# Expert steps of a streaming encoder kernel: six equal matmul pieces per row block, turns on VectorE, two neighbouring down rows per partition

## What is computed

```python
def swiglu(h, wg, wu, wd):
    g = jnp.einsum('btd,df->btf', h, wg)
    u = jnp.einsum('btd,df->btf', h, wu)
    return jnp.einsum('btf,fd->btd', jax.nn.silu(g) * u, wd)

def moe(h, router, wg, wu, wd):
    logits = jnp.einsum('btd,de->bte', h, router).astype(jnp.float32)
    vals, idx = lax.top_k(logits, TOP_K)
    gates = jax.nn.softmax(vals, axis=-1)
    comb = jnp.sum(jax.nn.one_hot(idx, N_EXPERTS, dtype=jnp.float32) * gates[..., None], axis=-2)
    for e in range(N_EXPERTS):
        out = out + comb[..., e:e + 1].astype(h.dtype) * swiglu(h, wg[e], wu[e], wd[e])
```

## Time and profile before

| | us |
|---|---|
| median of 3 runs | 1261.35 (1259.78 to 1263.61) |
| the profiled execution's own time | 1260.88 |
| its span, first to last instruction | 1259.0 |
| PE busy | 1235.7 (98%) |
| DVE busy | 316.3 (25%) |
| ACT busy | 303.8 (24%) |
| 277 MB of expert weights begin to be used at | 517 |
| one step of the loop, from SP's issues | 91.5 |

### The profile page before, as it was taken

How to read it: one execution, slowest core, us unless ns; L and a number is a source line. 1 busy time by engine, 2 the same in 40 slices (tenths; PEclk the granted TensorE clock), 3 DMA queues, 4 the chain that set the end, 5 groups by cost and what they waited for, 6 DMA issues and landing times.

```text
span 1259.0 us, 30642 instructions
## 1 busy us (share of the span) xinstructions
PE 1235.7 (98%) x13657; PEld 909.0 (72%) x13657; DVE 316.3 (25%) x640; ACT 303.8 (24%) x594; POOL 79.0 (6%) x175
## 2 busy tenths in 40 slices
PE   8999999999999999999999999999999999999998
PEld 5476699999975656667677676676676676675775
DVE  1677544444326566200000000000000000000002
ACT  2566533333334654200100100100101101001001
POOL 4231000000001020000000000100100100000100
PEclk9999999999999999999999999999999999999999
DMA  8261385544050632999999999999999999999991
GB/s 293 50 164 34 101 267 168 167 151 165 20 197 1 128 102 88 390 394 408 398 382 404 398 379 394 394 382 393 390 381 395 386 388 396 386 387 389 384 365 52
DMA packets 124224, 349.70 MB, mean 278 GB/s; under 512 B 8400, under 2 KB 33840, under 8 KB 124096
## 3 DMA queue, kind: packets, MB, share of 16 engines
q1 hardware_dynamic: 118896, 335.55, 72.1%
q0 software_dynamic: 3648, 10.60, 3.0%
q10 hardware_dynamic: 1552, 1.56, 0.4%
HBM read 339.65 MB, written 8.04 MB: 276 GB/s over the span
## 4 chain that ended last, share of the span: by engine, by line
PE 92%; DVE 3%; DMA 2%; ACT 2%; issue 1%; SPq 0%; DVEq 0%; ACTq 0%
PE ps L2307 33%; PE ps L2312 22%; PE ps L2219 11%; PE ps L1963 8%; PE ps L2235 5%; DMA ring<-in_w_in 2%; PE ps L2332 1%; PE ps L2036 1%; PE ps L2044 1%; PE ps L2096 1%; PE ps L2111 1%; PE ps L2149 1%; PE ps L2159 1%; PE ps L1976 1%; PE ps L2060 1%
## 5 line engine op out<-in xcount | busy, mean ns | idle before, releaser
L2307 PE MATMUL ps<-ring,xg 128*32 128x512 f32 (+2 forms) x2688 | 279.1, 465 | 7.4 <-issue 7.4
L2312 PE MATMUL ps<-ring,xg 128*32 128x256 f32 (+1 forms) x1344 | 276.5, 365 | 0.0
L2307 PE MATMUL ps<-ring_more,xg 128*32 128x512 f32 (+2 forms) x1920 | 196.6, 454 | 0.0
L2312 PE MATMUL ps<-ring_more,xg 128*32 128x256 f32 (+1 forms) x960 | 193.6, 358 | 0.0
L2312 PEld LDWEIGHTS ps<-ring,xg 128*32 128x32 f32 x1344 | 147.5, 110 | 37.0 <-issue 0.2
L2307 PEld LDWEIGHTS ps<-ring,xg 128*32 128x32 f32 x2688 | 118.7, 110 | 48.3 <-issue 14.0
L1762 DVE TENSOR_TENSOR act_m<-sgm,ps 128x768 f32<-128x768 f32 x24 | 22.9, 954 | 473.6 <-PE ps L2312 473.6
L2312 PE MATMUL ps<-ring_more,am 128*32 128x256 f32 x636 | 140.1, 379 | 0.0
L2307 PE MATMUL ps<-ring_more,am 128*32 128x512 f32 (+1 forms) x1272 | 139.8, 486 | 0.0
L2312 PEld LDWEIGHTS ps<-ring_more,xg 128*32 128x32 f32 x960 | 103.6, 110 | 27.7
L1963 PE MATMUL ps<-ring,hT 128*128 128x512 f32 x256 | 115.3, 596 | 0.1
(11 more groups left out here) (360 smaller groups left out, 1570.1 us busy)
## 6 DMA issues: line engine op xcount, KB each, us to landing
ring<-in_moe_w_up SPq DMA_DIRECT2D x48, 1024.0 KB, 11.6
ring_more<-in_moe_w_down SPq DMA_DIRECT2D x48, 1024.0 KB, 8.7
ring<-in_moe_w_gate SPq DMA_DIRECT2D x32, 1024.0 KB, 8.2
ring_more<-in_moe_w_gate SPq DMA_DIRECT2D x32, 1024.0 KB, 9.4
ring<-in_moe_w_down SPq DMA_DIRECT2D x32, 1024.0 KB
ring_more<-in_moe_w_gate SPq DMA_DIRECT2D x32, 768.0 KB, 9.6
ring<-in_moe_w_up SPq DMA_DIRECT2D x32, 768.0 KB, 7.6
ring_more<-in_moe_w_up SPq DMA_DIRECT2D x16, 1024.0 KB, 8.0
```

The lines of the kernel that those rows point to most:

```text
L2307: ins = mm_(ps[GRAN * g:GRAN * g + GRAN, b + c0 // 512, 0:c1 - c0], x[:, GRAN * g:GRAN * g + GRAN], w[:, c0:c1], start=first, stop=last)
L2312: ins = mm_(ps[SLOTS:P, b + c0 // 512, at_:at_ + tail], x[:, GRAN * g:GRAN * g + GRAN], w[:, main:main + tail], start=(first and g == here ...
```

## The change

- **Pieces.** `granules` takes the place of `lanes` for gate, up and, in the loop, down. Each row block gets six matmuls of the same length (half the chunk's columns: 512, or 384 in chunk 2). Granules 0 and 1 have two quarters each, one for each half of the columns, all in one bank (`fixed`). Granule 2's two halves go to the next bank (`shared`), on quarters 0 and 1 for even row blocks and on 2 and 3 for odd ones, so that two partial sums stand in four quarters. Over two row blocks each tile streams 1536 columns, as before. The last step's down stays with `lanes`.
- **Partial sums.** ACT copies the upper half of granule 2's partial sum to SBUF (`gate_part`, `up_part`, `y_tail`), DVE adds the lower one (`gates`, `activations`, `output`), and silu and product run in two pieces.
- **Turns.** `turn_chunk` and `turn_rows` are gone from PE, and the copies behind them from ACT and DVE. DVE writes `am` and `xg` with 32x32 transposes, SBUF to SBUF: 12 a chunk (`turned`) and 12 for the tokens (`tokens`), of 32 partitions by 256 elements (192 in chunk 2).
- **Down rows.** Partition p now holds hidden rows p·nk to p·nk+nk-1 of a chunk (nk is 8, in chunk 2 it is 6), so the two row blocks of a unit are one run of 8 KB for each partition. The transposes read `act_m` with a step of nk to match.

```diff
+                def granules(b, x, w, half, n, n_last):
+                    def fixed():
+                        for s_ in range(4):
+                            g, h = s_ // 2, s_ % 2
+                            ins = mm_(ps[GRAN * s_:GRAN * s_ + GRAN, b, 0:half], x[:, GRAN * g:GRAN * g + GRAN], w[:, half * h:half * h + half],
+                                      start=(n == 0), stop=(n == n_last))
+                        return ins
+                    def shared():
+                        for h in range(2):
+                            r0 = GRAN * (2 * (n % 2) + h)
+                            ins = mm_(ps[r0:r0 + GRAN, b + 1, 0:half], x[:, GRAN * 2:SLOTS], w[:, half * h:half * h + half],
+                                      start=(n < 2), stop=(n >= n_last - 1))
+                        return ins
+                    if n % 2:
+                        shared()
+                        return fixed()
+                    fixed()
+                    return shared()
...
-                    k0 = CW // P * c + sum(KUNIT[c][0:h])
-                    src = a["moe_w_down"][0].rearrange("e (k p) n -> p (e k) n", p=P)[:, bass.ds(e * FT + k0, n), :]
+                    k0 = sum(KUNIT[c][0:h])
+                    chunk = a["moe_w_down"][0, bass.ds(e, 1), CW * c:CW * c + WIDTH[c], :]
+                    src = chunk.rearrange("o (p k) n -> p (o k) n", k=nk)[:, k0:k0 + n, :]
...
 # ACT
-                    A(sgm[:, 0:ACT_W[c]], wide(0)[:, 0:ACT_W[c]], ACT.Silu).then_inc(silu_done, 1)
+                    A(sgm[0:HALF, BANK:BANK + w], ps[HALF:P, 1, 0:w], ACT.Copy).then_inc(gate_part, 1)
+                    A(sgm[:, 0:w], ps[:, 0, 0:w], ACT.Silu)
+                    act.wait_ge(gate_sum, j * CHUNKS + (c + 1))
+                    A(sgm[0:HALF, BANK:BANK + w], sgm[0:HALF, BANK:BANK + w], ACT.Silu).then_inc(silu_done, 1)
...
 # DVE
+                    V.tensor_tensor(part, part, ps[0:HALF, 3, 0:w], ALU.add).then_inc(up_sum, 1)
+                    V.tensor_tensor(act_m[:, 0:w], sgm[:, 0:w], ps[:, 2, 0:w], ALU.mult)
+                    dve.wait_ge(up_sum, j * CHUNKS + (c + 1))
+                    V.tensor_tensor(part, part, sgm[0:HALF, BANK:BANK + w], ALU.mult).then_inc(act_done, 1)
...
+                    for g, h, r0, c0, _ in streams(c):
+                        for q in (2 * h, 2 * h + 1):
+                            c1 = c0 + GRAN * nk * (q % 2)
+                            src = act_m[r0:r0 + GRAN, c1:c1 + GRAN * nk].rearrange("p (i k) -> p k i", k=nk)
+                            ins = V.transpose(am[GRAN * q:GRAN * q + GRAN, c % 2, 0:nk, GRAN * g:GRAN * g + GRAN], src)
+                    ins.then_inc(am_ready, 1)
...
+                    dve.wait_ge(xr_full, 16 * (j + 1))
+                    for g in range(MAIN):
+                        rows = xr[GRAN * g:GRAN * g + GRAN, :].rearrange("p (k c) -> p k c", c=P)
+                        for q in range(P // GRAN):
+                            ins = V.transpose(xg[GRAN * q:GRAN * q + GRAN, :, GRAN * g:GRAN * g + GRAN], rows[:, :, GRAN * q:GRAN * q + GRAN])
+                    ins.then_inc(xg_ready, 1)
```

More of the change, by code:

```diff
@@ L63 @@
 HALF = P // 2
[L64 to L67, removed]
+BANK = 512
 D_TAIL = D // (MAIN + 1)
@@ L558, in wide, with streams @@
             return ps[0:rows, b:b + 2, :].rearrange("p a b -> p (a b)")
[L560 to L579, removed]
+        def streams(c):
+            half = WIDTH[c] // 2
+            return [(s_ // 2, s_ % 2, GRAN * (s_ % 4), BANK * (s_ // 4), half) for s_ in range(2 * MAIN)]
         def wait_full(eng, key):
@@ L2264, in table @@
                 ins.then_inc(table_full, 1)
-            def turn_rows(count):
-                pe.wait_ge(xr_full, 16 * (count - 1))
-                for k in range(KD):
-                    ins = tr(ps[:, 4 + k // 4, (k % 4) * P:(k % 4) * P + SLOTS], xr[0:SLOTS, k * P:(k + 1) * P], ident[0:SLOTS, 0:SLOTS])
-                ins.then_inc(xgT_full, 1)
             busy(ps[:, 0, :], 1, 4 * P)
@@ L2364, in expert @@
                 pe.wait_ge(silu_done, j * CHUNKS + 1)
-                project("gate", 1, 0)
-                project("gate", 1, 1)
-                if not final:
-                    pe.wait_ge(table_out, j + 2)
-                turn_chunk(0)
-                project("gate", 1, 2)
-                project("gate", 1, 3)
+                for h in range(4):
+                    project("gate", 1, h)
+                pe.wait_ge(act_done, j * CHUNKS + 1)
                 for h in range(4):
@@ L2378, in expert @@
                 pe.wait_ge(silu_done, j * CHUNKS + 2)
-                project("gate", 2, 0)
-                project("gate", 2, 1)
-                turn_chunk(1)
-                project("gate", 2, 2)
-                project("gate", 2, 3)
+                for h in range(4):
+                    project("gate", 2, h)
+                pe.wait_ge(act_done, j * CHUNKS + 2)
                 for h in range(4):
@@ L2386, in expert @@
                 wait_turned(1)
-                if not final:
-                    turn_rows(j + 2)
-                down(1, 0)
-                down(1, 1)
-                if not final:
-                    pe.wait_ge(xg_high, j + 2)
-                    pe.wait_ge(xg_ready, j + 2)
-                turn_chunk(2)
-                down(1, 2)
-                down(1, 3)
+                for h in range(4):
+                    down(1, h)
                 wait_turned(2)
```

127 lines of the change are left out of this document (68 added, 59 removed).

## The result

The changed kernel takes 1218.04 us (median of 4 runs, 1216.69 to 1219.62), the kernel before 1261.62 beside it (1259.78 to 1263.61): ratio 0.966, 95% interval 0.9648 to 0.9673. That is 43.6 us faster. The direction was right; the size was not: 1228.6 was forecast, and 1222 was the low end of the range. The profiled execution of after took 1219.62 us with a span of 1217.8, so 41.3 us of the difference stand in the two traces that are compared here.

A forecast was written before the change was run, and what follows sets the result against it. PE was taken to set the pace, with the weights coming just as fast. 1260.9 us less 31.2 for turns and 1.1 for fewer matmuls, with 0 for transposes and supply, gave 1228.6 us; range 1222 to 1242.

The forecast's parts named there:

- What bounds the kernel: Expert stage: PE sets the pace at 2.59 us a unit, weights come just as fast, DMA has little room.
- Turns off PE: Loop steps: removing the turn matmuls from PE saves 31.2 us, bounds 29.6 and 32.6, or 4.0 us a step.
- The table, the turn of the loop, and the jump out of the loop with its 2.83 us gap stay.: PE's loop and exit: these costs outside the streaming were taken to remain, so no gain was counted for them.
- Six pieces for nine: Row blocks on PE: a third fewer matmuls with the same columns saves 1.1 us, range 0 to 5.3.
- Transposes covered: End of a step: DVE's transposes, 0.36 and 0.42 us each, finish at 11.5 us, under 18.1; price zero.
- The weights' supply: DMA over the steps: supply 89.2 us against PE's 87.4, deficit 1.8 a step, just covered by the lead; price 0.
- (a): DMA: supply takes over, long packets no better or 6% slower, 1234 or 1246 us, still faster; chance 0.18.
- cushion: Weights' lead: 13.1 us at the first steps, plus some 3 us of last-step gap that PE alone pays.
- (b): DMA: supply makes the kernel slower than before, down packets over 13% slower; 1296 us at 30%; chance 0.03.
- (c): End of a step: transposes at three times a copy make PE wait 12.2 us a step, 1314 us; chance 0.05.
- (d): Row blocks: shared matmuls keep other tiles waiting, up to 0.43 us a block, 1450 us; chance 0.02.

The follow-up runs named there:

- seven-piece run: The changed kernel with one of the two shared matmuls of each row block cut in two by columns, seven matmuls for six: 1229.39 us, ratio 0.9757.
- eight pieces: The changed kernel with both shared matmuls of each row block cut in two by columns, eight matmuls for six: 1230.19 us, ratio 0.975.
- 4 KB rows: The changed kernel with down weights back to one row per partition and transposes reading neighbouring elements: 1222.3 us, ratio 0.970.
- the run with the cut turns: The kernel before with each turn on PE cut to its first matmul, output not the reference's: 1237.87 us, ratio 0.9815.
- twelve pieces: The changed kernel with all six matmuls of each row block cut in two by columns, twelve for six: 1251.81 us, ratio 0.992.
- the first move of `sum_rows`: The changed kernel with POOL's load of `sum_rows` issued behind the use of unit 29 of the last step: 1217.06 us, ratio 0.9657.

## Why the prediction was too high

**What bounds the kernel.** Right: PE set the pace with the supply close behind, and both stayed so.

**Turns off PE.** Right. 32.6 us by the delays was the upper bound and fits the account; 31.2 was 1.4 too careful.

**"The table, the turn of the loop, and the jump out of the loop with its 2.83 us gap stay."** This is the step that failed. The gaps of the turn and the exit did not stay, and with the half clock behind the exit that is 7.6 + 4.5 = 12.1 us, more than the whole miss of 10.6. (The table did stay, at 0.74 us for 0.94.) I had read "issue" as a property of the loop. The page of before had its own row against that, 114 instruction packets, and I didn't ask what they were for; nor did I count PE's instructions a step. The order of the two kernels shows a third fewer expert matmuls on PE; I priced that by streaming alone. For the turn's 7.6 us the run on before without the quarter-3 pieces shows that the shorter body is the cause, and the seven-piece run that one piece more loses it again. For the exit's 4.5 us the runs show less: the same run on before has them gone with nothing but fewer matmuls, but with seven and eight pieces they stay gone although the body is fetched. What took that gap away remains open.

**Six pieces for nine.** Right in kind: 2.6 us as the remainder of the account, 1.9 by the pace of the row blocks, against 1.1, inside the range of 0 to 5.3. No run shows the 5.3 us; it was my estimate of how far the pace could fall, and the runs showed the 1.9 to 2.6 in its place. The stretch from 620 to 1100 us of after and of before shows fewer matmuls, no idle time, and more data moved in the same time:

```profile
620.00:1100.00 480.00, 480.00 (x4760) 1.00 1.02 404
```

```profile
620.00:1100.00 480.00, 476.50 (x6788) 1.00 1.02 390
```

**Transposes covered.** The price of zero was right, with less room than I wrote. DVE by shape (busy, mean ns), after:

```profile
L1774 DVE STREAM_TRANSPOSE am<-act_m 32x256 f32<-32x256 f32 x192 | 123.1, 641 | 2.7
L1783 DVE STREAM_TRANSPOSE xg<-xr 32x256 f32<-32x256 f32 x84 | 36.6, 435 | 1.3
L1774 DVE STREAM_TRANSPOSE am<-act_m 32x192 f32<-32x192 f32 x96 | 49.5, 515 | 2.0
```

I had 0.42 and 0.36. The tokens, read with unit step, cost 0.435; the chunks of `act_m`, read with a step of eight elements, 0.641, half as much again for the same shape. The end of a step is 2.1 + 12 x 0.515 + 12 x 0.435 = 13.5 us against 18.1, so 4.6 us of slack where I had 6.6. The trace puts both places closer:

```profile
673.38 6.35 DVE L1774 STREAM_TRANSPOSE am<-act_m 32x192 f32<-32x192 f32 x12
679.76 5.37 DVE L1783 STREAM_TRANSPOSE xg<-xr 32x256 f32<-32x256 f32 x12
```

The tokens are ready at 685.1, 3.9 us ahead of the next step at 688.99. The tightest place is the one before it, which I had with 4.0 us (6.4 against 10.4): chunk 2 of `am` is ready at 679.7, and down 2 begins with it at 681.26, 1.5 us later. Transposes some quarter slower would have used that up in each step. With 4 KB rows, where the step is one, the same engine has:

```profile
L1774 DVE STREAM_TRANSPOSE am<-act_m 32x128 f32<-32x128 f32 x384 | 116.1, 302 | 5.3
```

The two forms differ in the price of an element: with unit step 128 elements took 302 ns and 256 took 435, so the second 128 cost only 133, about 1.0 ns an element over a fixed part of some 170. Strided, from 192 to 256 elements it is 126 ns, about 2.0 an element.

**The weights' supply.** The model held, its price of zero did not. 8 KB packets took 313 ns at the median, close to the 309 of the line through 3 and 4 KB, so rival (a), slower long packets, is out. Unit 18 of steps 1 and 5 (lengths, issue, time to landing), against the earlier trace rows:

```profile
L718 SPq DMA_DIRECT2D ring_more<-in_moe_w_down x1: 333/333/333, 621.7 to 621.7; - x1
DMA to landing us min/median/max: 18.1/18.1/18.1
```

```profile
L718 SPq DMA_DIRECT2D ring_more<-in_moe_w_down x2: 878/942/1005, 969.2 to 970.4; - x2
DMA to landing us min/median/max: 21.1/22.4/23.3
```

(969.2 + 21.1 - 621.7 - 18.1) / 4 = 87.6 us of supply for a step, where I had 89.2, against PE's 85.74, where I had 87.4. The deficit is 1.9 a step, and 1.8 was predicted: two errors of the same sign and size. The lead at unit 18, from its landing to PE's first matmul with it, fell from 12.5 us in step 0 to 3.0 in step 5 and 1.2 in step 6, where the shortest one was 0.9 us. What I had left out were two things of the last step: the load of `sum_rows`, 2.8 us of DMA just there, and the exit's gap, which I counted as 3 us of cushion and which was gone. So the supply cost 4.2 us and 1.7 of half clock, where the sum had 0. This took back half of what the vanished gaps had given. That the total missed by only 10.6 us is in part luck: without the supply's cost it would have been some 16.

**Sum of the misses**, in the direction of the sum: turns -1.4, loop and exit -12.1, streaming -1.5, supply +5.9, start +0.4: -8.7, against -9.0 between 1228.6 and the profiled 1219.6.

**Rivals.** (a) happened in a small form, 5.9 us in the last step, by the melted lead and the load of the sums and not by the packets. (b), (c) and (d) did not: no DVE wait in the steps, and the undisturbed stretch shows no block above its pace.

## What to carry to other kernels

Where a loop on PE shows "issue" gaps at its turn or exit, count the loop body's instructions and look at the instruction queue's packets: here bodies of 1754 stayed, bodies of 1972 or more were fetched in each step and had 0.4 to 2.7 us of gap a step by it, so a change that crosses this line is worth more, or costs more, than its columns. When two resources are within 3% of each other, follow the lead over all steps to the last one and list every other load that falls where it is smallest. Of the longest idle gaps on PE in the expert stage (2.26 us and more) seven of nine cost 1.7 us or more besides by the clock, so one long wait can be dearer than three short ones of the same sum. And when a run of yours hits its expected number, check the parts too: the run with the cut turns hit its 1238 with two errors that cancelled.

## What the runs showed of the hardware

- **Loop body on PE.** It was held at 1692 and 1754 instructions, with no instruction packet from step 0 to the exit, and fetched as a whole from 1972 on. Where it was fetched, a packet started 3.2 to 3.4 us after the branch and PE went on 5.6 to 6.0 us after it. What exactly sets the limit between 1754 and 1972, why the exit takes half a us longer, and what decides how many matmuls are at hand there, stays open.
- **Clock.** In the expert stage PE's granted clock fell to 0.50 for about 3.4 us behind idle gaps of 2.83 (before), 3.56 (after), 2.26, 2.28, 2.30 and 2.38 us (twelve pieces), and for 6.8 us around the end of a gap of 4.01 us in the same run, 5.05 of them with PE at work. It stayed at 1.00 behind gaps of 2.29 and 2.66 us in that same twelve-piece run, of 2.0 (seven pieces) and 2.2 (4 KB rows). So no length of gap alone decides it: none up to 2.2 did it, and from 2.26 to 2.66 both occur. In the run with the first move of `sum_rows` and in that with eight pieces it fell once at the start of step 0, for 3.4 us, with no gap over 0.4 us close before it, and made that step 87.46 and 87.66 us. This is not explained.
- **DMA.** 3, 4 and 8 KB packets of weights took 125, 162 and 313 ns at the median in after (the quickest tenth 121, 159 and 309) on each of 16 engines, with up to 426 GB/s in a stretch of 8 us (1096 to 1104).

- **VectorE.** 32x32 transposes of f32 cost 435 ns for 256 elements a partition with unit step, 641 with a step of eight. GpSimd's operations in the steps took as long beside them as before (fetching the rows 972 ns for 976, adding them 1464 for 1465).
